# Three-block transformer kernel: expert blocks with all 24 quarters split, gate biases as a one-hot product on TensorE, and the first row block's blanking on SyncE's queue

## The reference

```python
def clamped_swiglu_expert(xb, w_gu, b_gu, w_dn, b_dn):
    gu = xb @ w_gu + b_gu
    gate = jnp.minimum(gu[:, :D_FF_3], SWIGLU_LIMIT)
    up = jnp.clip(gu[:, D_FF_3:], -SWIGLU_LIMIT, SWIGLU_LIMIT)
    glu = gate * jax.nn.sigmoid(SWIGLU_ALPHA * gate)
    return ((up + 1.0) * glu) @ w_dn + b_dn
...
    yb = lax.map(run_block, (xb, blk_e)).reshape(P, D)
    y = jax.ops.segment_sum(yb * row_gate[:, None].astype(yb.dtype), row_tok, num_segments=N)
```

## Time and profile before

| | us |
|---|---|
| median of 3 runs | 3319.97 (3319.68 to 3324.28) |
| the profiled execution's own time | 3321.52 |
| its span, first to last instruction | 3319.7 |
| busy in the span: PE / DVE / ACT / POOL | 3104.9 / 1830.9 / 1596.4 / 737.2 |

### The profile page before, as it was taken

One profiled execution on the slowest core, in us unless ns is written; L12 is line 12 of the kernel. 1 busy time (PEld: TensorE's weight loads), 2 busy tenths in 40 slices (PEclk: granted clock), 3 DMA queues, 4 the chain that ended last, 5 costly groups with the idle time before them and its releaser, 6 DMA issues. The chain is left out here.

```text
span 3319.7 us, 39152 instructions
## 1 busy us (share of the span) xinstructions
PE 3104.9 (94%) x14036; PEld 2408.6 (73%) x14036; DVE 1830.9 (55%) x2216; ACT 1596.4 (48%) x2141; POOL 737.2 (22%) x379
## 2 busy tenths in 40 slices
PE   7986999998999999989997888999999999999997
PEld 6754678877877787768885666777777777777753
DVE  3257433344367404440031447887888888888773
ACT  4334434433566423232231325766766766666652
POOL 2400144442523344324442330000000000000020
PEclk9987999999999999999998898999999999999998
DMA  3243322222222132212224317999999999999971
GB/s 148 102 161 119 127 76 101 101 89 89 77 76 76 52 114 77 102 51 101 89 108 191 153 51 318 402 408 411 406 407 412 405 408 411 406 407 411 411 262 45
DMA packets 65594, 693.72 MB, mean 209 GB/s; under 512 B 6912, under 2 KB 7296, under 8 KB 25440
## 3 DMA queue, kind: packets, MB, share of 16 engines
q1 hardware_dynamic: 54336, 650.05, 49.8%
q0 software_dynamic: 6912, 25.17, 2.0%
q10 hardware_dynamic: 4256, 17.30, 1.3%
HBM read 654.22 MB, written 38.27 MB: 209 GB/s over the span
## 5 line engine op out<-in xcount | busy, mean ns | idle before, releaser
L142 POOL TENSOR_TENSOR ring_low<-ring,mix_ring_high 128x1024 fp32r<-128x1024 f32 x120 | 292.4, 2470 | 455.2 <-ACT mix_ring_high L137 455.2
L213 PE MATMUL psum<-mix_high,mix_ring_high 128*128 128x512 f32 x864 | 342.9, 397 | 13.1 <-DVE h_low L507 8.6
L215 PE MATMUL psum<-mix_high,ring_low 128*128 128x512 f32 x864 | 337.1, 390 | 0.0
L213 PE MATMUL psum<-ex_high,ex_rows_high 128*128 128x512 f32 x768 | 314.9, 410 | 1.5 <-DVE ex_rows_low L2823 1.4
L215 PE MATMUL psum<-ex_high,ex_rows_low 128*128 128x512 f32 x768 | 299.7, 390 | 0.0
L214 PE MATMUL psum<-h_low,mix_ring_high 128*128 128x512 f32 x736 | 287.2, 390 | 0.0
L142 POOL TENSOR_TENSOR ring_low<-ring,ff_ring_high 128x1024 fp32r<-128x1024 f32 x72 | 175.0, 2464 | 415.0 <-ACT ff_ring_high L137 224.7
L2510 POOL CAST ex_index<-table 128x1 uint32 (+1 forms) x32 | 5.9, 184 | 1090.2 <-PE psum L2550 1032.5
L2854 DVE TENSOR_TENSOR ring_low<-ring,ex_high 128x2048 fp32r<-128x2048 f32 x96 | 214.4, 2287 | 38.7 <-ACT ex_high L2686 38.6
L2854 DVE TENSOR_TENSOR ex_more_low<-ex_more,ex_high_in_x 128x2048 fp32r<-128x2048 f32 x96 | 219.5, 2287 | 19.9 <-ACT ex_high_in_x L2686 19.9
L2605 PE MATMUL psum<-ex_more,ex_act_t 128*128 128x512 f32 x512 | 224.9, 592 | 0.0
(11 more groups left out here) (581 smaller groups left out, 6884.8 us busy)
## 6 DMA issues: line engine op xcount, KB each, us to landing
ex_more<-moe_w SPq DMA_DIRECT2D x128, 2048.0 KB, 9.3
ring<-wstream SPq DMA_DIRECT2D x87, 2048.0 KB, 8.4
ring<-moe_w SPq DMA_DIRECT2D x64, 2048.0 KB, 10.5
ex_bias_up<-moe_b SPq DMA_DIRECT2D x32, 1024.0 KB, 9.6
y_rows<-mx_zero ACTq DMA_DIRECT2D x1, 16384.0 KB, 44.5
y_rows<-ex_y SPq DMA_DIRECT2D x32, 512.0 KB, 10.5
x<-xt SPq DMA_DIRECT2D x8, 256.0 KB, 6.1
rel<-rel_bias SPq DMA_DIRECT2D x1, 2048.0 KB, 9.7
```

Source lines behind the costliest of these rows:

```text
L142: e.tensor_tensor(low, full, high.bitcast(F32), ALU.subtract).then_inc(self.low_ready, 1)
L213: pe.matmul(out, a[0], b[0], start=start, stop=False)
L215: return pe.matmul(out, a[1], b[0], start=False, stop=stop)
```

## The change

1. In `expert_stage` the second halves of pieces 4 and 5 are split like the others: 24 quarters, 12 low pairs, no full fp32 matmuls; the ring of high parts has 12 slots, two of them in the place of the tile `h`. PE's last four quarters are (4,2), (4,3), (5,2), (5,3). `act_high` and `act_low` hold eight tiles; there are two `low_act` on DVE and two `high_act` on ACT.
2. The gate bias no longer is added by DVE. A tile `gate_bias` holds the gate biases of all 32 experts, high parts on partitions 0 to 31 and low parts on 32 to 63; POOL makes `picks_bias`, a one-hot 64x128 tile for the expert of the next block, and PE opens each of the two gate banks with one matmul of 512 columns by it. ACT's Silu reads the gate bank in PSUM; the limit is taken on the Silu's result, in DVE's last operation of `take_up`. `take_gate` is gone. The factor 1/1.702 moves into `take_y`.
3. The bias DMA of a block has half its size (up biases alone). The table is loaded once at the start of the stage (two DMAs of 128 KB ahead of the weights on SP's queue), ACT copies it ahead of the norm's root, DVE makes the low half after the norm. The opening has six more small DVE operations (`owner`), and ACT waits at n = 10 for the store of the tokens.
4. In `mixer_stage` the blanking of row block 0 moves from ACT's queue to the end of SP's, after its last panel load and ahead of the stage's wait.

```diff
@@ mixer_stage, SP and ACT
                 ring.load_until(sp, min(n0 + 4 + SLOTS, FIRST["ple_proj"]))
+                sp.wait_ge(zeroed, 1)
+                sp.dma_start(r.y_dram[0:ROWS, :], zero[:, :]).then_inc(r.blanked, 16)
                 sp.wait_ge(r.blanked, 32)
...
-                act.dma_start(r.y_dram[0:ROWS, :], zero[:, :]).then_inc(r.blanked, 16)
                 norm.preload(act)
                 norm.root(act)
@@ expert_stage
-    RING = 10
-    PIECES = tuple((s, c) for s in range(4) for c in range(PARTS)) + tuple((s, c) for s in (4, 5) for c in range(2))
+    RING = 12
+    PIECES = tuple((s, c) for s in range(4) for c in range(PARTS)) + tuple((s, c) for half in (0, 2) for s in (4, 5) for c in (half, half + 1))
...
-    act_at, dve_at = (8, 14), (10, 14, 18)
+    act_at, dve_at = (8, 16), (16, 22)
@@ SP
+                for i in range(2):
+                    sp.dma_start(bias_raw[i * NE:(i + 1) * NE, :], g.extra["moe_b"][:, 0:D]).then_inc(bias_in, 16)
...
-                    sp.dma_start(bias_up[:, :], g.extra["moe_b"][e, 0:2 * D].partition_broadcast(P)
+                    sp.dma_start(bias_up, g.extra["moe_b"][e, D:2 * D].partition_broadcast(P)
...
-                        if s < 4:
-                            sp.wait_ge(used, b * NQ + place[s, PARTS - 1] + 1)
-                        else:
-                            sp.wait_ge(dn_done, b * 2 + s - 3)
+                        sp.wait_ge(used, b * NQ + place[s, PARTS - 1] + 1)
@@ POOL
+                def pick_bias(after, at):
+                    pool.wait_ge(used, after * NQ + NQ + place[2, 0] + 1)
+                    pool.tensor_copy(picks_bias[:, :], owner[:, at].to_broadcast([2 * NE, P])).then_inc(picks_set, 1)
+                    pool.wait_ge(picks_set, after + 2)
...
                     gather(b + 1, bass.ds(b + 1, 1))
+                    pick_bias(b, bass.ds(b + 1, 1))
@@ PE
+                    pe.wait_ge(picks_set, b + 1)
                     for s in range(4):
-                        pe.wait_ge(taken, b * 4 + s + 1)
+                        pe.wait_ge(up_taken if s % 2 else gate_taken, b * 2 + s // 2 + 1)
+                        if s % 2 == 0:
+                            pe.matmul(psum[:, s, :], picks_bias[:, :], gate_bias[:, 256 * s:256 * s + 512], start=True, stop=False)
...
-                    pe.wait_ge(a_ready, b + 1)
+                    pe.wait_ge(a_low, b * 2 + 2)
                     for s in (4, 5):
-                        for k in range(4, KT):
-                            mm = pe.matmul(psum[:, s + 2, :], act_t[:, k - 4, :], weights(s, k), start=False, stop=k == KT - 1)
-                        mm.then_inc(dn_done, 1)
+                        for c in range(2, PARTS):
+                            quarter(b, s, c, psum[:, s + 2, :], act_high, act_low)
@@ ACT
                 def sigmoid(b, c):
-                    act.wait_ge(limited, b * 2 + c + 1)
+                    act.wait_ge(used, b * NQ + NQ + place[2 * c, PARTS - 1] + 1)
                     act.wait_ge(h_done, b * 2 + c + 2)
-                    act.activation(sig[:, :], gate[:, :], ACT.Silu, scale=SW_ALPHA).then_inc(sig_ready, 1)
+                    act.activation(sig[:, :], psum[:, 2 * c, :], ACT.Silu, scale=SW_ALPHA).then_inc(gate_taken, 1)
...
+                        if opening and n == 10:
+                            act.wait_ge(x_stored, 16)
...
                 norm.preload(act)
+                act.wait_ge(bias_in, 32)
+                act.activation(gate_bias[:, :], bias_raw[:, :], ACT.Copy).then_inc(bias_high, 1)
                 norm.root(act)
@@ DVE
+                    for i, ends in enumerate((first, upto)):
+                        link(dve.tensor_tensor(owned[:, :], ends[:, :], stacked[:, :], ALU.mult))
+                        link(dve.tensor_reduce(owner_first[:, i:i + 1], owned[:, :], AX_X, ALU.add))
+                    iota = g.block_iota[0:2 * NE, :]
+                    link(dve.tensor_scalar(owner[:, :], iota, owner_first[0:2 * NE, 1:2], None, ALU.is_lt))
+                    dve.scalar_tensor_tensor(owner[:, :], iota, owner_first[0:2 * NE, 0:1], owner[:, :], ALU.is_ge, ALU.mult).then_inc(owner_set, 1)
...
-                def take_gate(b, c):
-                    dve.wait_ge(used, b * NQ + NQ + place[2 * c, PARTS - 1] + 1)
-                    dve.wait_ge(up_in, b * 16 + 16)
-                    dve.tensor_tensor(gate[:, :], psum[:, 2 * c, :], bias_up[:, 512 * c:512 * c + 512], ALU.add).then_inc(taken, 1)
-                    dve.wait_ge(taken, b * 4 + 2 * c + 5)
-                    dve.tensor_scalar(gate[:, :], gate[:, :], SW_LIMIT, None, ALU.min).then_inc(limited, 1)
...
-                    dve.scalar_tensor_tensor(act_rows[:, c, :], up[:, :], 1.0 / SW_ALPHA, sig[:, :], ALU.mult, ALU.mult).then_inc(h_done, 1)
+                    dve.scalar_tensor_tensor(act_rows[:, c, :], sig[:, :], SILU_LIMIT, up[:, :], ALU.min, ALU.mult).then_inc(h_done, 1)
...
                         if n == dve_at[0]:
-                            take_gate(b, 0)
+                            take_up(b, 0)
                         if n == dve_at[1]:
-                            take_up(b, 0)
-                        if n == dve_at[2]:
-                            take_gate(b, 1)
+                            low_act(b, 0)
                         low_pair(b, n)
...
-                    low_act(b)
                     take_up(b, 1)
-                    for c in range(2):
-                        low_rows(b * 2 + 2 + c, c, 5)
+                    low_rows(b * 2 + 2, 0, 5)
+                    low_act(b, 1)
+                    low_rows(b * 2 + 3, 1, 5)
```

More of the change, by code:

```diff
@@ L208, in with_low, with __init__, tile @@
     return t, nc.alloc_sbuf_tensor_at(f"{name}_low", shape, F32R, offset=at)
+class Places:
+    def __init__(self, nc, name, at, room):
+        self.nc, self.name, self.at, self.end = nc, name, at, at + room
+    def tile(self, name, shape, dtype=F32):
+        t = self.nc.alloc_sbuf_tensor_at(f"{self.name}_{name}", shape, dtype, offset=self.at)
+        self.at += -(-4 * int(np.prod(shape[1:])) // 32) * 32
+        assert self.at <= self.end
+        return t
 def split_product(pe, out, a, b, start, stop):
@@ L2402, in expert_stage @@
         low_piece = lambda s: g.ring.low[:, s, :] if s < SLOTS else more_low[:, s - SLOTS, :]
-        weights = lambda s, k: piece(s)[:, k * PANEL:(k + 1) * PANEL]
         def slots(n, count):
             n %= RING
-            at = high[:, n:n + count, :] if n < 6 else high_in_x[:, n - 6:n - 6 + count, :]
+            tile, n = (high, n) if n < 6 else (high_in_x, n - 6) if n < 10 else (high_in_h, n - 10)
+            at = tile[:, n:n + count, :]
             return at.rearrange("p a f -> p (a f)")
-        gate = nc.alloc_sbuf_tensor_at("ex_gate", [P, 512], F32, offset=g.neg_head_at)
         up = nc.alloc_sbuf_tensor_at("ex_up", [P, 512], F32, offset=g.sums_at)
@@ L2433, in expert_stage @@
         neg_top, chosen, total = sb("neg_top", [P, TT]), sb("chosen", [P, TT, NE]), sb("total", [P, TT])
-        e_sel, inv = r.e_sel, r.inv
-        count, blocks, upto, first, ones_e = (sb(n, [P, NE]) for n in ("count", "blocks", "upto", "first", "ones_e"))
-        top_dest, first_rank = sb("top_dest", [P, TT, 8]), sb("first_rank", [P, TT])
-        token, token_f = sb("token", [P, TT], I32), sb("token_f", [P, TT])
-        at_i, row_i, row_of, block_of_choice = sb("at_i", [P, NC], I32), sb("row_i", [P, NC], I32), sb("row_of", [P, NC]), sb("block_of_choice", [P, NC])
@@ L2439, in expert_stage @@
-        seen, block_of = sb("seen", [P, NE]), sb("block_of", [P, 1])
-        norm = norm(sem, r.bias_up[:, :].rearrange("p (a s) -> p a s", a=4))
+        e_sel, inv, ones_e = r.e_sel, r.inv, sb("ones_e", [P, NE])
+        count, blocks, upto, first, seen = (after_parts.tile(n, [P, NE]) for n in ("count", "blocks", "upto", "first", "seen"))
+        top_dest, first_rank = after_parts.tile("top_dest", [P, TT, 8]), after_parts.tile("first_rank", [P, TT])
+        token, token_f, block_of = sb("token", [P, TT], I32), sb("token_f", [P, TT]), sb("block_of", [P, 1])
@@ new lines, in expert_stage @@
+        at_i, row_i = after_parts.tile("at_i", [P, NC], I32), after_parts.tile("row_i", [P, NC], I32)
+        row_of, block_of_choice = after_parts.tile("row_of", [P, NC]), after_parts.tile("block_of_choice", [P, NC])
+        owned, owner, owner_first = after_parts.tile("owned", [P, NE]), sb("owner", [2 * NE, TABLE]), after_parts.tile("owner_first", [P, 2])
+        picks_bias = sb("picks_bias", [2 * NE, P], F32R)
+        bias_raw = inside("bias_raw", [2 * NE, D], g.starts_at)
+        norm = norm(sem, r.bias[:, 0:S].rearrange("p (a s) -> p a s", a=1))
@@ L2566, in quarter @@
                                            (slots(n, 1)[:, j * PANEL:(j + 1) * PANEL],
-                                            low_piece(s)[:, k * PANEL:(k + 1) * PANEL]), k == 0, k == KT - 1)
```

(1 more changed line is left out.)

79 lines of the change are left out of this document (45 added, 34 removed).

## The result

The changed kernel takes 3292.89 us (median of 4 runs, 3289.73 to 3294.53) against 3319.97: 0.9914 of before, 95% interval 0.9897 to 0.9931. It is faster, by 27 us, and not by the 57 forecast; the time lies outside the predicted range. The profiled execution took 3292.72 us, with a span of 3290.9.

A forecast was written before the change was run, and what follows sets the result against it. The loop was taken as bound by PE's matmuls. From the profiled 3321.52 us, -31.4 - 27.3 + 1.0 + 1.1 = -56.6 gave 3264.9; the median, 1.55 lower, was forecast at 3263.4 us, range 3257 to 3282.

The forecast's parts named there:

- Blanking: Mixer stage's opening: with the second blanking issue off ACT's queue, the reciprocal starts at 1804.1, not 1835.45, saving 31.4 us.
- SP's small store: Row block 0's 512 KB store on SP lands in 2.6 us, hidden by 0.3 us; if not, up to 1 us.
- The loop: Expert loop on PE: period from 35.96 to 35.08 us, 0.88 saved per block, 27.3 us in all (24.2 to 30.1).
- the bias matmuls: PE in the loop: two added per block at 0.27 us each, between 0.227 and 0.32, together 0.54 us.
- DVE as the bound: Expert loop: DVE's own cycle of 34.55 to about 34.7 us follows PE's 35.08; as rival it binds, chance 0.17.
- The rival at 3279: Expert loop: handovers, POOL's copy and slower low pairs make DVE bind, period 35.6, 16 us more; chance 0.17.
- POOL's copy: Expert loop: POOL's new copy can hold DVE up on shared ports, costing at most 0.3 us a block.
- The weights: Expert loop: rival where weights land too late; 9.3 us expected, up to 14.6 costs nothing; slower than before, chance 0.03.
- a wait of ACT for a `moe_w` landing: Sign in the changed profile that would speak for the rival of late weights, chance 0.03.
- The expert stage's opening: ACT's root waits for two table DMAs and the copy: cost 1.0 us (0.3 to 1.7; up to 3 if late).
- Block 0: First expert block: six small DVE operations come ahead and block 1 starts later, cost 1.1 us (0 to 2.5).
- The last stage: Tail after PE's end: the same `take_y` and store as before, so unchanged, 0 us.

The follow-up runs named there:

- experiment 4: The changed kernel with its bias matmul over 32 partitions in place of 64, the table's low part left out of the result: 3295.32 us, single run.
- experiment 8: The changed kernel without bias matmuls and with one matmul in place of three for each piece of panel 5: 3254.6 us, single run.
- experiment 7: For block 0: the changed kernel with the six `owner` operations moved to the end of DVE's block 0, 3291.93 us; two further kernels under this number.
- the kernel with the increments: The changed kernel with 64 semaphore increments on POOL between its loop and the last stage: 3289.85 us.
- experiment 9: The one with all four edits, plus nine throw-away turns on PE in the router's two waits: 3261.81 us.
- the one with all four edits: The changed kernel with 128-row bias matmuls, root ahead of the table's copy, 64 POOL increments, and `owner` operations at block 0's end: 3264.14 us.

## Why the prediction was wrong

**Blanking: right.** -31.4 us was said. The stall is 31.3 us shorter by the marks; alone the moved line is worth 30.8 us by the times, as 0.7 are given back up to `n_blocks`. Neither the third panel's load nor SP's small store cost anything at the end. The store's term was wrong all the same: it landed 10.9 us after its issue and not 2.6, and still 1.3 us ahead of the end of POOL's last work in the stage.

**The loop: the bias matmuls were mis-sized, and this is the step that failed.** Predicted 0.27 us each, bounds 0.227 to 0.32; measured 0.63. 2 x (0.63 - 0.27) x 31 = 22.3 us, against 27.3 - 5.9 = 21.4 missed in the loop. The other terms held: with two matmuls of 128 rows, the plain step each, the sum gives 34.99 and the measured period is 35.01; 31 x (35.96 - 35.01) = 29.5 us are saved. The bound came from the pair of 96-row matmuls in the earlier trace rows, and it misled twice. Its 0.32 is no step: the first of the pair is shown starting under the last turn, and the two cost 0.23 us each. And 96 rows stood for 64, which behave otherwise (experiment 4). The way from 128 to 64 rows was in the trace of the kernel before, at L1742, with its 0.32 us and its load that comes late, but in no row that I read. The prediction named this as what would make it wrong ("if bias matmuls cost much more than 0.32") but priced no case for it.

**DVE as the bound: it isn't.** Its cycle was put at 34.55 to 34.7 us; experiment 8 measured 34.56. The rival at 3279 has no part in the result, though the time lies on its side: in the changed kernel's loop PE never waits for DVE. Low pairs out of the slots in `h` take 2.28 us as the others do. POOL's copy stretches one low pair from 2.28 to 2.38 us, inside the 0.3 allowed.

**The weights: no, though their sign is there.** `ex_more` lands in 10.4 us (median) and not 9.3, under the 14.6 from which it would have cost. The prediction named a wait of ACT for a `moe_w` landing as what would speak for late weights, and the changed kernel has it (waits in 2100 to 3000: total, times, longest):

```profile
ACT ex_high_in_x L2714 <- DMA ex_more<-moe_w: 39.3, 23, 2.4
```

No wait of PE stands in the same view, so it costs nothing: the sign was too weak for what it was to show.

**The expert stage's opening: +2.9 us and not +1.0.** The tables landed 4.0 us (median) after issues at 1966.8 and 1967.3, where 2.0 to 3.3 were taken, so the root was 3 us late, the upper end that I had named. That putting the root first doesn't pay was unforeseen: the clock took it.

**Block 0: +1.5 and not +1.1.** The six operations cost 1.4 by experiment 7, where 1.3 were summed; that is nearly all of it.

**The last stage: +3.6 and not 0.** I had written that the tail was unchanged, which is true of its work and not of POOL's code ahead of it. 2.4 are the first gather's delay. About 1 us is left, which the kernel with the increments still has (0.9), experiment 9 too (0.7), and the one with all four edits has not. It goes with the granted clock. Window views of 8 us show 0.57 in the changed kernel (3206 to 3214) and 0.79 with 128 rows (3182 to 3190), which is the lower level for 6.9 and 3.4 us. Over all traces: where from the first gather to the end 0.7 to 1.9 us are lost against the kernel before, the clock is low for 6.8 us between 30 and 50 us into the stage, in one piece or two (seven kernels); where it is 0.6 or less, for 3.4 us (the other five, and the kernel before). No run changes this alone, so that the clock is the cause is likely and not shown.

**Sum.** Missed: loop 21.4, stall 0.1 and what was given back behind it 0.7, opening 1.9, block 0 0.4, tail 3.6, together 28.1, less 0.3 for the start and the rest: 27.8 = 3292.7 - 3264.9, the profiled execution against its own forecast.

## What to carry to other kernels

In a stream of 128-row matmuls one of 64 or 32 rows is not a small one: fill it to 128 rows with zeros, and look at whether its weight load starts under the matmul ahead of it. When the nearest row for a new operation has another row count or other neighbours, look through the whole trace for one with the same, price the way in and out too, or give the unknown a rival of its own. Where a change has several parts, the smallest may hold all of the gain: here one moved DMA issue gave 31 us, and the rewritten loop paid only once its bias matmuls had 128 rows. A repaired stall on PE's feeder is worth what PE's clock leaves of it.

## What was not expected of the hardware

- A 64-row matmul between 128-row ones costs 0.63 us instead of 0.227, 32 rows 0.66; two in a row pay the extra 0.40 once (0.41). The weight loads on both sides of it are not pulled ahead. Two 96-row ones between turns and 128-row ones cost 0.23 us each, with their loads pulled ahead.
- 64 semaphore increments on an idle POOL brought its next DMA issue 2.4 us forward.
- Nine useless turns on PE made the router's part 2.5 us shorter: the clock stood at its lower level for 3.4 us in place of about 10.
- ACT's second DMA issue behind a 16 MB blanking held it for 31.86 us; the same store issued on SP held nobody.
